# Expert front of two MoE layers: raw rows transposed, the row factor applied to the logits, the gather in fp32 by four chunks

## The reference, cut to what matters

```
h = rms_norm(x, norm_ffn) * (1 + scale_f) + shift_f
grp_prob = softmax(h @ w_router_grp + b_router_grp)        # 4 groups, top 1
exp_logits = h @ w_router_exp + b_router_exp               # 8 experts a group
sel = exp_logits of the chosen group; top 2; weights softmax(top 2) * grp_w
y = sum over chosen experts e: w_e * (silu(h @ w_gate[e]) * (h @ w_up[e])) @ w_down[e]
x = x + gate_f * y
```

## Time and profile before

| | us |
|---|---|
| median of 3 runs | 1499.07 (1498.95 to 1501.53) |
| the profiled execution | 1498.55 |
| its span, first to last instruction | 1496.4 |

### The profile page before, as it was taken

How to read it: one execution, slowest core, us unless ns; L and a number is a source line. 1 busy time by engine, 2 the same in 40 slices (tenths; PEclk the granted TensorE clock), 3 DMA queues, 4 the chain that set the end, 5 groups by cost and what they waited for, 6 DMA issues and landing times. The chain is left out here.

```text
span 1496.4 us, 21265 instructions
## 1 busy us (share of the span) xinstructions
PE 1315.1 (88%) x8922; PEld 966.2 (65%) x8922; DVE 736.0 (49%) x1122; ACT 539.1 (36%) x914; POOL 50.8 (3%) x46
## 2 busy tenths in 40 slices
PE   6999998566579999976556899999999999999997
PEld 2766765233237667632223678889998878799986
DVE  1745663112146457522111677765545777765554
ACT  3535441000034445200000445654443546654443
POOL 0200000000002000000000101000000110000000
PEclk9999999888899999998788999999999999999999
DMA  9898879999987957799999724346655405445551
GB/s 354 288 333 283 297 302 422 421 420 422 418 304 272 338 181 298 318 421 421 422 421 419 216 62 169 131 140 200 199 197 168 111 1 174 164 149 193 194 190 50
DMA packets 135976, 392.10 MB, mean 262 GB/s; under 512 B 26816, under 2 KB 40128, under 8 KB 111296
## 3 DMA queue, kind: packets, MB, share of 16 engines
q1 hardware_dynamic: 132128, 389.48, 70.2%
q10 hardware_dynamic: 3744, 1.15, 0.4%
HBM read 389.45 MB, written 1.05 MB: 261 GB/s over the span
## 5 line engine op out<-in xcount | busy, mean ns | idle before, releaser
L412 DVE TENSOR_TENSOR spl<-ring,spl 128x2048 fp32r<-128x2048 f32 x65 | 149.3, 2297 | 136.5 <-ACT spl L403 136.5
L527 PE MATMUL ps<-hh,spl 128*128 128x256 f32 x1728 | 206.9, 281 | 2.8 <-DVE hh L490 2.8
L527 PEld LDWEIGHTS ps<-hh,spl 128*128 128x128 f32 x1728 | 204.9, 189 | 6.9 <-issue 5.8
L1290 PE MATMUL ps<-spl_as_slots,ar 128*32 128x256 f32 x1184 | 135.3, 504 | 73.0 <-DMA spl_as_slots<-in_w_up 26.7
L403 ACT ACTIVATE spl<-ring 128x2048 fp32r<-128x2048 f32 x66 | 126.6, 1919 | 152.3 <-PE ps L527 108.6
L2271 PE MATMUL ps<-spl,ur 128*128 128x512 f32 x768 | 176.7, 389 | 0.0
L2271 PEld LDWEIGHTS ps<-spl,ur 128*128 128x128 f32 x768 | 143.2, 188 | 29.2
L897 DVE TENSOR_TENSOR spl<-ring,spl 128x1024 fp32r<-128x1024 f32 (+2 forms) x120 | 138.3, 1175 | 21.9 <-ACT spl L888 21.5
L1290 PEld LDWEIGHTS ps<-spl_as_slots,ar 128*32 128x32 f32 x1184 | 66.9, 143 | 116.6 <-issue 106.3
L888 ACT ACTIVATE spl<-ring 128x1024 fp32r<-128x1024 f32 (+2 forms) x120 | 116.9, 1011 | 46.3 <-DMA ring<-in_w_in 11.2
L1504 DVE TENSOR_TENSOR ar<-ps,ar 128x256 f32<-128x256 f32 x16 | 6.8, 425 | 253.7 <-ACT ar L1378 253.7
(11 more groups left out here) (367 smaller groups left out, 1808.7 us busy)
## 6 DMA issues: line engine op xcount, KB each, us to landing
ring<-in_w_down SPq DMA_DIRECT2D x62, 1024.0 KB, 6.1
ring<-in_w_ada SPq DMA_DIRECT2D x48, 1024.0 KB, 7.2
spl_as_slots<-in_w_up SPq DMA_DIRECT2D x46, 1024.0 KB, 16.5
ring<-in_w_up SPq DMA_DIRECT2D x40, 1024.0 KB, 5.2
ring<-in_w_in SPq DMA_DIRECT2D x34, 1024.0 KB, 7.7
ring<-in_w_gate SPq DMA_DIRECT2D x34, 1024.0 KB, 15.9
...
```

The source lines that it names most:

```text
L412: v.tensor_tensor(t.lo, t.raw, t.hi, ALU.subtract).then_inc(s_lo, 1)
L527: ins = pe.matmul(ps[:, banks[m // 2], (m % 2) * 256:(m % 2) * 256 + 256], le, ri, start=(kk == 0 and q == 0 and m % 2 == 0), stop=(kk == ...
L1290: ins = pe.matmul(ps[32 * j:32 * j + 32, 2 + q % 2, 256 * z:256 * z + 256], mo.xg[:, e // 16, k, 32 * (e % 16):32 * (e % 16) + 32], T[("ga ...
```

## The change

- **Rows turned raw.** TensorE transposes the rows of x itself, half by half, as soon as a half is complete, without filler matmuls ahead. ScalarE scales four 128x128 blocks of half 0, VectorE three groups of four blocks at once. No shift is added.
- **Row factor late.** The router has tokens on partitions: the scaled block is stationary, the 36 columns of `rw` move, so no turn of the logits follows. The row factor multiplies the logits on VectorE together with the bias. The part of the logits that comes from the shift is computed once a layer: `dve_router_shift` on VectorE ahead of the row adds, and a product with ones on TensorE. The second half's norm moves behind the selection; the last square of ScalarE moves behind its four blocks.
- **fp32 gather.** The gather reads `xn` itself in fp32, stationary side `xn[:, i, k::8]`, two matmuls per k and chunk in place of four; the split into two parts goes. Chunks are 128, 128, 256 and 512 slots. `mo.pr` is plain fp32 and lies elsewhere; the weighted places go to another buffer, since `xn` stays in use.
- **Order of TensorE.** Gather 0, gate 0, up 0, gather 1, turn 0, down 0, gate 1, gather 2, up 1, turned places, scatter 0, turn 1, down 1, gather 3, gate 2, and so on. The copies of the turned places and the PSUM copies of chunks 2 and 3 move accordingly on ScalarE and VectorE.
- `dve_rest` and `pe_rest` put the row factor and the shift back for the branch of overfull experts.

The diff, without lines that only rename semaphores or move buffers (context lines left out):

```diff
@@ -447,11 +448,14 @@
-        def dve_norm(v, g, event, parts=None):
+        def dve_norm_half(v, g, i):
+            v.wait_ge(*g(s_rs))
+            v.tensor_scalar(xn[:, i, :], x[:, i, :], st[:, 2 + i:3 + i], None, ALU.mult).then_inc(s_xn, 1)
...
@@ -873,7 +877,7 @@
-            act_rows(sc, 2 * l + 1, [(i, c) for i in range(2) for c in range(2)], g)
+            act_rows(sc, 2 * l + 1, [(0, 0), (0, 1), (1, 0)], g)
...
@@ -1013,6 +1017,7 @@
+            dve_router_shift(v, l)
...
@@ -1181,10 +1186,11 @@
-        mo.pr = ur[:, 8192:10240].rearrange("p (i n) -> p i n", i=2)
+        mo.pr = carve(8192, 2, 1024)
-        mo.pw = xn
-        mo.lgt, mo.lT = carve(U_N + 3584, 2, 36), carve(U_N + 3664, 256)[0:36, :]
+        mo.pw = hf[:, 2048:4096].rearrange("p (i n) -> p i n", i=2)
+        mo.lgt, mo.bias = carve(U_N + 3584, 2, 36), carve(U_N + 3664, 36)
+        mo.srw, mo.srs = carve(U_N + 2048, 8, 36), carve(U_N + 2048 + 288, 36)
...
@@ -1203,64 +1207,80 @@
-        CHUNKS = [(0, 256), (256, 256), (512, 512)]
+        CHUNKS = [(0, 128), (128, 128), (256, 256), (512, 512)]
+        def rw(l):
+            return PR(f"rw{l}").rearrange("p (k n) -> p k n", k=8)
-            if c == 0:
-                eng.wait_ge((s_xga, s_xgd)[k // 2 % 2], 10 * l + k // 4 + 1)
+            if c < 3:
+                eng.wait_ge((s_xga, s_xgd)[k // 2 % 2], 10 * l + 2 * c + k // 4 + 1)
-                eng.wait_ge((s_xga, s_xgd)[k % 2], 10 * l + 4 * c - 2 + k // 2 + 1)
+                eng.wait_ge((s_xga, s_xgd)[k % 2], 10 * l + 6 + k // 2 + 1)
+        def turned_rows(i, k):
+            return ps[:, (3, 0)[i] + k // 4, 128 * (k % 4):128 * (k % 4) + 128]
+        def pe_router_rows(pe, l, i):
+            pe.wait_ge(s_x, 8 * l + 2 + 2 * i)
+            for k in range(8):
+                ins = pe.transpose(turned_rows(i, k), x[:, i, k::8], ident)
+                if k % 4 == 3:
+                    ins.then_inc(s_rT, 1)
+        def pe_router(pe, l, i, ks):
+            for k in ks:
+                if i == 0 and k < 4:
+                    pe.wait_ge(s_ra, 4 * l + k + 1)
+                elif k % 4 == 0:
+                    pe.wait_ge(s_rd, 3 * l + 2 * i + k // 4)
+                ins = pe.matmul(ps[:, 7, 36 * i:36 * i + 36], mo.stage[:, k, 128 * i:128 * i + 128], rw(l)[:, k, :], start=(k == 0),
+                                stop=(k == 7), skip_group_check=True)
+            return ins
-            pe_spin(pe, 7, 4)
-            pe.wait_ge(*g(s_xn, 2))
-            pe_rows_T(pe, xn)
-            rw = PR(f"rw{l}").rearrange("p (k n) -> p k n", k=8)
-            for k in range(8):
-                if k % 2 == 0:
-                    pe.wait_ge(*g(s_hT))
-                ins = pe.matmul(ps[0:36, 4, 0:256], rw[:, k, :], mo.stage[:, k, :], start=(k == 0), stop=(k == 7))
-            ins.then_inc(s_rt[0], 1)
-            pe.wait_ge(*g(s_rt[1]))
-            for i in range(2):
-                ins = pe.transpose(ps[:, 5, i * 36:i * 36 + 36], mo.lT[:, i * 128:(i + 1) * 128], ident[0:36, 0:36])
-            ins.then_inc(s_rt[2], 1)
+            pe.wait_ge(s_bs, 2 * l + 1)
+            pe.matmul(ps[:, 6, 256:292], C("ones"), mo.srs, start=True, stop=True).then_inc(s_bs, 1)
+            pe_router_rows(pe, l, 0)
+            pe_router(pe, l, 0, (0, 1))
+            pe_router_rows(pe, l, 1)
+            pe_router(pe, l, 0, range(2, 8))
+            pe_router(pe, l, 1, range(8)).then_inc(s_lg, 1)
-            pe.wait_ge(*g(s_rt[3]))
+            pe.wait_ge(s_pk, l + 1)
-            pe.matmul(mo.cum[:, 2, :], C("ones"), mo.pick[:, 1, :], start=False, stop=True).then_inc(s_rt[4], 1)
+            pe.matmul(mo.cum[:, 2, :], C("ones"), mo.pick[:, 1, :], start=False, stop=True).then_inc(s_cum, 1)
-            pe.wait_ge(s_pl, 3 * l + 1)
-            for k in range(8):
-                pe_gather(pe, l, 0, k)
+            pe.wait_ge(*g(s_xn, 2))
+            pe_gather(pe, l, 0)
-            pe.wait_ge(s_pl, 3 * l + 2)
-            for k in range(8):
-                pe_gather(pe, l, 1, k)
+            pe_gather(pe, l, 1)
-            pe.wait_ge(s_pl, 3 * l + 3)
-            for k in range(8):
-                pe_gather(pe, l, 2, k)
+            pe_gather(pe, l, 2)
+            pe_gate_up(pe, l, 1, 1)
-                slots_ready(pe, l, 2, 4 + m)
+                slots_ready(pe, l, 2, 2 * m + 1)
-            for q in range(1, 7):
-                if q > 1:
-                    pe_gate_up(pe, l, q, 0)
+            pe_scatter(pe, l, 0)
+            pe_turn(pe, l, 1)
+            pe_down(pe, l, 1)
+            pe_gather(pe, l, 3)
+            for q in range(2, 7):
+                pe_gate_up(pe, l, q, 0)
...
@@ -1273,15 +1293,22 @@
-        def pe_gather(pe, l, c, k):
+        def slots_out(c, k):
+            n = CHUNKS[c][1]
+            return ps[:, 4 + k % 4, 0:n] if c == 3 else ps[:, 4 + k // 2, 256 * (k % 2):256 * (k % 2) + n]
+        def pe_gather(pe, l, c):
-            if c and k > 3:
-                slots_ready(pe, l, c, k - 4)
-            o = ps[:, 4 + k % 4, 0:n] if c else ps[:, 4 + k // 2, 256 * (k % 2):256 * (k % 2) + 256]
-            for q, (i, z) in enumerate(((0, 0), (0, 1), (1, 0), (1, 1))):
-                ins = pe.matmul(o, mo.xs[z][:, i, k, :], mo.pr[:, i, s0:s0 + n], start=(q == 0), stop=(q == 3), skip_group_check=True)
-            if c or k % 2:
-                ins.then_inc(s_ga, 1)
+            pe.wait_ge(s_pl, 4 * l + c + 1)
+            for k in range(8):
+                if c == 3 and k == 2:
+                    pe.wait_ge(s_bo, 28 * l + 4)
+                if c == 3 and k > 3:
+                    slots_ready(pe, l, c, k - 4)
+                for i in range(2):
+                    ins = pe.matmul(slots_out(c, k), xn[:, i, k::8], mo.pr[:, i, s0:s0 + n], start=(i == 0), stop=(i == 1), skip_group_check=True)
+                if c == 3 or k % 2:
+                    ins.then_inc(s_ga, 1)
...
@@ -1299,9 +1326,12 @@
-                if q == 1:
-                    slots_ready(pe, l, 1, 6)
-                    slots_ready(pe, l, 1, 7)
+                if q in (1, 2):
+                    slots_ready(pe, l, q, 5)
+                    slots_ready(pe, l, q, 7)
+                if q == 4:
+                    slots_ready(pe, l, 3, 6)
+                    slots_ready(pe, l, 3, 7)
...
@@ -1310,11 +1340,13 @@
-                slots_ready(pe, l, 1, 4)
+                slots_ready(pe, l, 1, 1)
+            if q in (2, 3):
+                slots_ready(pe, l, 3, q + 2)
...
@@ -1343,6 +1375,8 @@
+                if q == 1 and m < 2:
+                    slots_ready(pe, l, 3, 6 + m)
...
@@ -1351,16 +1385,12 @@
-            act_rows_hi(sc, l, 0)
-            for k2 in range(4):
-                sc.wait_ge(*g(s_xT))
-                k = 2 * k2
-                sc.activation(mo.stage[:, k, :], ps[:, k2, 0:256], ACT.Identity, scale=aff[:, 2, k:k + 1], bias=aff[:, 3, k:k + 1]).then_inc(s_st, 1)
-            act_rows_hi(sc, l, 1)
-            sc.wait_ge(*g(s_rt[0]))
-            sc.activation(mo.lT, ps[0:36, 4, 0:256], ACT.Copy).then_inc(s_rt[1], 1)
-            sc.wait_ge(*g(s_rt[5]))
-            sc.activation(mo.et, mo.et, ACT.Exp).then_inc(s_rt[6], 1)
+            sc.wait_ge(s_rT, 4 * l + 1)
+            for k in range(4):
+                sc.activation(mo.stage[:, k, 0:128], turned_rows(0, k), ACT.Identity, scale=aff[:, 2, k:k + 1]).then_inc(s_ra, 1)
+            act_rows(sc, 2 * l + 1, [(1, 1)], g, 3)
+            sc.wait_ge(s_et, l + 1)
+            sc.activation(mo.et, mo.et, ACT.Exp).then_inc(s_ete, 1)
...
@@ -1379,18 +1409,19 @@
-                    for k in (0, 2, 4, 6):
+                    for k in (0, 1, 4, 5):
+                if q == 1:
+                    for m in (0, 2):
+                        sc.wait_ge(s_pT, 4 * l + m + 1)
+                        sc.activation(mo.pT[:, 2 * m:2 * m + 2, :], ps[:, 4 + m, :].rearrange("p (q n) -> p q n", q=2), ACT.Copy).then_inc(s_pTa, 1)
-                if q == 0:
-                    for k in (0, 2, 4, 6):
-                        act_slots(sc, l, 2, k)
-                    for m in (0, 2):
-                        sc.wait_ge(s_pT, 4 * l + m + 1)
-                        sc.activation(mo.pT[:, 2 * m:2 * m + 2, :], ps[:, 4 + m, :].rearrange("p (q n) -> p q n", q=2), ACT.Copy).then_inc(s_pTa, 1)
+                if q < 2:
+                    for k in ((0, 1, 4, 5), (0, 2, 4, 6))[q]:
+                        act_slots(sc, l, 2 + q, k)
...
@@ -1442,20 +1464,30 @@
+        def dve_router_shift(v, l):
+            v.wait_ge(s_adf, ada_n[l, 6] + 1)
+            v.wait_ge(*own_dve(v.tensor_tensor(mo.srw, rw(l), bc(aff[:, 3, :], 2, 36), ALU.mult)))
+            v.tensor_reduce(mo.srs, mo.srw.rearrange("p k n -> p n k"), AX.X, ALU.add).then_inc(s_bs, 1)
-            dve_norm(v, g, 2 * l + 1)
-            dve_rows_lo(v, l, 0)
-            for k2 in range(4):
-                v.wait_ge(*g(s_st))
-                k = 2 * k2 + 1
```

(54 more changed lines are left out.)

39 lines of the change are left out of this document (17 added, 22 removed).

## The result

The changed kernel takes 1505.48 us (median of 12 runs, 1501.93 to 1509.04) against 1499.01 us before in the same series (12 runs, 1495.48 to 1506.49): a ratio of 1.0043 with a 95% interval of 1.0028 to 1.0057. It is **slower** by 6.5 us, a small difference, but clear of the noise. Forecast were 1488.5 us and a range up to 1493.5. The profiled execution of the changed kernel took 1502.41 us, its span is 1500.2.

What follows compares the result with a forecast made beforehand. Full DMA engines bound the expert stage, so the queue's restart sets its end: 5.0 + 0.27 + 0.19 = 5.46 us earlier, less 0.15, gives 5.3 a layer, 10.6 in all: 1488.5 us, range 1485.5 to 1493.5.

Steps and rivals of the forecast that it cites:

- What bounds the kernel: Expert stage: DMA engines are full, so 1 us earlier at the queue's restart is 1 us earlier at stage end.
- Router: From the last row add to the copy of the group logits: 5.0 us earlier, bounds 1.8 and 5.6.
- Places: Places of chunk 0 on VectorE shrink from 512 to 256 elements a partition: 0.27 us earlier.
- First gather: Gather of chunk 0 on TensorE: records of 0.12 us, 3.84 us against 4.03, so 0.19 us earlier.
- Time to the end of the third gate pass: TensorE's work from the queue's restart to that pass's end: 54.6 us, 46.0 before.
- limit of 55.8: Latest end of the third gate pass, in us after the restart, before the queue is held at tile 35.
- margin of 1.2 us: Room before the queue is held at tile 35; called small, so 0.15 us of loss a layer was taken.
- Rival 3: Strided fp32 loads not hidden, 0.19 us more per gather record: slower, 1534 us, break-even 0.052 us a record; chance 0.05.
- Rival 2: Strided stationary side costs at 128 columns, 0.165 us a record in chunks 0 and 1: 1491.4 us; chance 0.08.
- Rival 1: Queue held at tile 35, TensorE ending the third gate pass 2 to 4 us late: 1493.8 us; chance 0.12.
- The clock: TensorE at 1.2 GHz for the front's 6 us, costing up to 3 us a layer: 1494.5 us; chance 0.03.
- The sign the text had named: Prediction is wrong if a 128-column gather record is over 0.17 us or the DMA stands still a second time.

Runs made afterwards that it cites:

- e6: e2 with the matmuls of gather 0 issued twice, nothing else changed; 1495.94 us, ratio 0.9971 to the kernel before.
- e4: Changed kernel, strided read kept, with gather 3 moved behind the third gate pass; 1500.41 us, ratio 1.0001 to the kernel before.
- e2: Changed kernel with normalized rows stored with k outside, so the gather reads packed columns of the right features; 1488.56 us, ratio 0.9930 to the kernel before.
- e8: e2 with filler matmuls added before the gate and the up pass of the last set; 1487.37 us, ratio 0.9893 to the kernel before.
- e9: e2 with 56 fp32 matmuls and transposes, packed and strided, added behind gather 3 to time each form; one run, 1519.46 us.
- e5: e2 with gather 3 moved behind the gate pass of the third set; 1489.47 us, ratio 0.9906 to the kernel before.

## Why the prediction was wrong, point by point

- **What bounds the kernel: right.** The stage follows the restart as long as the queue is not held (e6: 3.6 us there, 3.4 and 3.2 us at its end), and a held queue is lost time (e4). One us for one us was a little too much: of e2's 5.8 us at the restart 4.8 arrive at the end of the stage, behind an up pass at the lower clock (e8).
- **Router, 5.0 us: right, 5.35.** A ScalarE block took 1.12/4 = 0.28 us instead of 0.36, which is 0.16 us for the two in the sum; most of the rest is the 0.3 us allowed until VectorE reads the logits, for which the rows show 0.04 (199.84 to 199.88). Places 0.27: right (0.42 us).
- **First gather, 3.84 us: this is the step that failed.** It took 7.86, four us more in front of the restart: 5.35 + 0.27 - 3.8 = 1.8, and 1.77 were measured. The text had both rows for the price, packed fp32 matmuls at 0.112 and strided transposes at 0.128, and went by the transpose because it had the stride. It was the wrong property to match by: e9 shows that the stride is nearly free in a transpose and doubles a matmul. None of the rows it had shows an fp32 matmul with a strided operand, so 0.112 and 0.128 were no bounds for the price.
- **Time to the end of the third gate pass, 54.6 us against a limit of 55.8.** With packed records it is 54.5 (e2): the sum and the order were right. With strided ones gather 1 is 4.05 longer, gather 2 0.9 and gather 3 0.1, so 59.6, and 59.56 was measured. The limit of 55.8 seems to hold as well, 59.56 - 55.8 = 3.8 us over it with 3.7 lost, but this is partly luck: the first hold had already set tile 34 back by 1.2 us, so the limit there was 57.0 by the text's own way. With 3.7 us lost it lay near 55.9, and near 54.7 without the first hold; the 54.5 of e2 just fits, and the margin of 1.2 us was hardly there.
- **The hold at tile 19: missing from the sum.** The same sum was due one step earlier, for the first down pass. In the changed kernel that pass starts 229.69 - 217.63 = 12.1 us after the restart, before it was 228.26 - 219.97 = 8.3, and the transfers lost 1.2 us. At the forecast records there is no hold (422 GB/s in 233 to 240 us of e2), so it cost the forecast nothing, but the sum should have had it.
- **The rivals.** Rival 3, the slower one, is what happened in its kind, not in its size. Its break-even was 0.052 us a record, and 0.12 came true, which is not the whole load in series (0.19). It also charged the extra to all chunks; chunk 2 paid 0.028 us and chunk 3 nothing, since more columns cover the load. Its formula with the true prices gives 5.46 - 4.0 for the restart and 4.1 + 0.9 + 0.1 - 1.2 = 3.9 for tile 35, 2.4 us a layer lost, and 3.6 with the hold at tile 19: 1504 to 1506 us. Rival 2 had the right mechanism with a price of 0.165. Between them they had 0.13; the row from the transposes should not have carried 0.68. Rival 1 (held at tile 35) happened, but as a consequence.
- **The clock: no part in it at the front.** It was granted 1.00 from 193 to 285 us in the changed kernel too. What e5 shows (0.59 for 3 us, 0.9 us lost) is the size of it when it does fall there.
- **The sign the text had named** (a 128-column record over 0.17 us, or a second standstill) came with both parts.
